# Delta rule, inverse of both directions: products first, then transpositions, then updates

## What is computed

```python
a_kk = jnp.where(strict, jnp.einsum("bhnid,bhnjd->bhnij", k_beta, k) * decay, 0.0)
eye = jnp.eye(c, dtype=q.dtype)
t_inv = lax.linalg.triangular_solve(eye + a_kk, jnp.broadcast_to(eye, a_kk.shape),
                                    left_side=True, lower=True, unit_diagonal=True)
u = jnp.einsum("bhnij,bhnjd->bhnid", t_inv, v * beta[..., None])
w = jnp.einsum("bhnij,bhnjd->bhnid", t_inv, k_beta * jnp.exp(gcum)[..., None])
```

## Time and profile before

| what | us |
|---|---|
| median of 3 runs | 2648.48 |
| lowest and highest of them | 2642.61, 2650.26 |
| span of the profiled execution, first to last instruction | 2645.5 |
| TensorE's busy time in it | 2556.8 |
| layer 0, step 0 levels | some 20 (1854.24 to 1874.16) |

### The profile page before, as it was taken

The page is one execution under the profiler, slowest core; times in us unless marked ns, Lnnn a source line. Parts: engine busy times, 40 slices in busy tenths (PEclk is TensorE's granted clock), DMA queues, the critical chain, the costliest instruction groups (busy, mean ns, idle before and its releaser), DMA issues.

```text
span 2645.5 us, 66516 instructions
## 1 busy us (share of the span) xinstructions
PE 2556.8 (97%) x30782; PEld 2085.4 (79%) x30782; DVE 1269.3 (48%) x1710; ACT 942.9 (36%) x1227; POOL 173.9 (7%) x178
## 2 busy tenths in 40 slices
PE   8999999999999999999999999998999999989999
PEld 7977799897786767767667765687779978877997
DVE  6677655556861000010100101388467857846785
ACT  4455443355540000000000000266545645654663
POOL 1000000000000000000000000202500000160000
PEclk9999999999999999999999999999999999999999
DMA  6445855554459999999999999743035445313443
GB/s 218 142 160 174 307 179 182 152 191 161 149 180 394 407 396 404 412 405 409 398 404 410 405 398 418 287 155 117 31 120 185 171 166 194 105 51 121 171 173 104
DMA packets 94362, 635.37 MB, mean 240 GB/s; under 512 B 11328, under 2 KB 12256, under 8 KB 24320
## 3 DMA queue, kind: packets, MB, share of 16 engines
q1 hardware_dynamic: 85392, 598.61, 59.0%
q0 software_dynamic: 7120, 29.70, 4.0%
q10 hardware_dynamic: 1568, 2.75, 0.3%
HBM read 626.17 MB, written 13.24 MB: 242 GB/s over the span
## 4 chain that ended last, share of the span: by engine, by line
PE 79%; DVE 11%; ACT 5%; issue 3%; DMA 3%; SPq 0%; DVEq 0%; ACTq 0%
PE ps L1032 31%; PE ps L756 13%; PE ps L758 13%; PE ps L757 13%; DVE wlo L1946 3%; DMA raw<-in_units_dram 3%; ACT whi L1481 2%; PE ps L1331 1%; ACT s L1829 1%; PE ps L1310 1%; PE ps L1342 1%; DVE s L2306 0%; DVE mx L2268 0%; DVE x L2381 0%; PE ps L964 0%
## 5 line engine op out<-in xcount | busy, mean ns | idle before, releaser
L1946 DVE TENSOR_TENSOR wlo<-raw,whi 128x2048 fp32r<-128x2048 f32 (+5 forms) x250 | 531.6, 2135 | 306.5 <-ACT whi L1481 306.0
L1032 PE MATMUL ps<-raw,xe 128*32 128x256 f32 x10752 | 585.3, 379 | 5.5 <-DMA raw<-in_units_dram 4.7
L1032 PEld LDWEIGHTS ps<-raw,xe 128*32 128x32 f32 x10752 | 391.1, 110 | 194.5 <-DMA raw<-in_units_dram 7.0
L1481 ACT ACTIVATE whi<-raw 128x2048 fp32r<-128x2048 f32 (+4 forms) x252 | 447.8, 1780 | 203.7 <-PE ps L758 188.8
L756 PE MATMUL ps<-xTh,whi 128*128 128x256 f32 x1480 | 418.1, 283 | 0.0
L758 PE MATMUL ps<-xTh,wlo 128*128 128x256 f32 x1480 | 417.4, 282 | 0.0
L757 PE MATMUL ps<-xTl,whi 128*128 128x256 f32 x1480 | 417.3, 282 | 0.0
L2489 DVE TENSOR_TENSOR hb<-ps,hb 128x384 f32<-128x384 f32 x56 | 31.2, 558 | 777.5 <-ACT hb L1656 777.5
L1032 PE MATMUL ps<-raw,hTe 128*32 128x256 f32 x5376 | 291.8, 379 | 3.5 <-issue 3.5
L756 PEld LDWEIGHTS ps<-xTh,whi 128*128 128x128 f32 x1480 | 279.1, 189 | 0.8 <-issue 0.7
L757 PEld LDWEIGHTS ps<-xTl,whi 128*128 128x128 f32 x1480 | 278.8, 188 | 0.1
(11 more groups left out here) (582 smaller groups left out, 3229.7 us busy)
## 6 DMA issues: line engine op xcount, KB each, us to landing
raw<-in_units_dram SPq DMA_DIRECT2D x544, 1024.0 KB, 7.7
raw<-in_units_dram SPq DMA_DIRECT2D x18, 512.0 KB, 3.5
raw<-in_units_dram SPq DMA_DIRECT2D x6, 768.0 KB, 6.9
raw<-in_units_dram SPq DMA_DIRECT2D x8, 544.0 KB, 3.6
raw<-in_units_dram SPq DMA_DIRECT2D x6, 688.0 KB, 4.0
g<-in_b_gate_dram POOLq DMA_DIRECT2D x16, 256.0 KB, 9.2
raw<-in_units_dram SPq DMA_DIRECT2D x4, 576.0 KB, 4.5
rows_y<-yb ACTq DMA_DIRECT2D x7, 288.0 KB, 6.4
```

The costliest lines, as they stand in the source:

```text
L1032: ins = self.e.matmul(bands(ps[r:r + 32, 256 * i:256 * i + 256]), G.x[:, kk, o:o + 32], w[:, k, :, c:c + 128], start=(kk == 0 and i != 1), ...
L1481: self.e.activation(self.m.hi[u % NHL][:, 0:n], self.m.raw[u % NRAW][:, 0:n], ACT.Copy) \
L1946: self.e.tensor_tensor(self.m.lo[u % NHL][:, 0:n], self.m.raw[u % NRAW][:, 0:n], self.m.hi[u % NHL][:, 0:n].bitcast(F32), ALU.subtract) \
```

## The change

The transposition `tr` becomes a step of its own behind the products of both directions. TensorE's queue in a level is then product 0, product 1, transposition 0, transposition 1, update 0, update 1. ScalarE's copies follow: `q` of 0, `q` of 1, `T` of 0, `T` of 1. VectorE, GpSimd and SyncE have nothing in the step `tr`. No instruction is added or taken away, and no semaphore wait changes its condition; the PSUM buffers are handed out in the new order.

```diff
@@ Plan.delta
-                o += [("lq", k) + c for c in K]
+                o += [("lq", k) + c for c in K] + [("tr", k) + c for c in K]
@@ Tensor.do
-        elif what in ("dd", "de", "kq", "gram", "qkT", "t0", "lq", "lu", "du", "s1", "s2"):
+        elif what in ("dd", "de", "kq", "gram", "qkT", "t0", "lq", "tr", "lu", "du", "s1", "s2"):
@@ Tensor.delta_inverse
                 ins = e.matmul(ps[half(a_), span(512 * c + 64 * r_)], m.E[d][r, s], TT[r, s], start=True, stop=True)
-            ins.then_inc(*self.up("mm_delta", ("full",) + key))
-            key = ("tr",) + a
+        elif what == "tr":
             ps = self.fill(key, ("T", k) + K)
             ins = self.turn_pairs(lambda r_: ps[:, span(128 * r_, 128)], TT)
@@ Scalar.do
-        elif what in ("dd", "de", "kq", "qkT", "t0", "lq", "du", "s2"):
+        elif what in ("dd", "de", "kq", "qkT", "t0", "lq", "tr", "du", "s2"):
```

## The result

| what | before | after |
|---|---|---|
| median of 20 runs, us | 2647.30 | 2654.32 |
| lowest and highest, us | 2642.61, 2651.72 | 2650.23, 2657.43 |
| span of the profiled execution, us | 2645.5 | 2654.2 |
| TensorE's busy time in it, us | 2556.8 | 2552.1 |

The ratio is 1.0025 with a 95% interval of 1.0020 to 1.0031: about 6.6 us slower (7.0 by the medians). Forecast were 3.2 us and a time of 2651.7. The time lies in the range and inside the 0.3% called no change, but the interval excludes a ratio of 1, and the size is twice the one forecast. That the time came within 2.6 us is in part luck: the forecast was counted from 2648.48, the median of three runs, and the median of the twenty is 2647.30.

What follows compares the result with a forecast made beforehand. TensorE's queue up to update 0 and the chain behind it were taken as the bound. Step 0 (1.07 and 0.77) and step 1 twice (1.36) made 3.2 us: 2648.48 to 2651.7 us, range 2644.5 to 2658.5.

Steps and rivals of the forecast that it cites:

- the ordinary level: Levels behind a step's first: ScalarE's copy sets update 0 at 2.62, so a level takes 4.12 us, 0.19 more.
- The first level: First level of a step: product 1 waits for `TT` of direction 1, update 0 comes 0.53 us later.
- the queue's saving of 0.34: TensorE's queue per level: two fewer tiling mode changes at 0.17 us each, left unused because ScalarE's copy comes last.
- step 0: Levels of step 0: 1.07 us longer in layer 0, 0.77 in layer 1.
- levels 2 and 3 nothing: Step 1, each layer: level 1 costs 0.30 us, levels 2 and 3 nothing, 4 and 5 0.19 each, 0.68 together.
- the halt gives back: Step 1: instruction halts of 0.65 and 0.81 us shrink by whatever a level loses inside a halted stretch.
- 3.62 us of a packet's way: Step 1: TensorE runs out of instructions, and an instruction packet's way takes at least 3.62 us.
- rival 1: All levels: the instruction supply hides the whole loss, time stays at 2648.5 us; chance 0.14.
- rival 2: All levels: saved mode changes count, 6.8 us less, or 1.6 less (2646.9) with the supply's floor; chance 0.06.
- rival 3: VectorE's subtractions stay 0.80 us apart, delaying product 1; each level loses 0.37, total 2657 us; chance 0.10.
- rival 4: TensorE's clock falls to 1.2 GHz because levels have idle gaps: 30 us more, 2682 us; chance 0.04.

Runs made afterwards that it cites:

- e7: All levels ordered product 0, transposition 0, transposition 1, product 1, against the kernel before: 2649.61 us, ratio 1.0009.
- e5: Changed kernel with only level 3 of step 1 back in the old order: 2650.49 us, ratio 1.0015 to the kernel before.
- e2: Kernel before with the new order in step 1 of both layers only: 2650.49 us, ratio 1.0012.
- e6: Kernel before with only level 3 of step 1 in the new order: 2652.97 us, ratio 1.0021.
- e9: Kernel before with only TensorE's queue in the new order, ScalarE's copies in the old: 2659.55 us, ratio 1.0037.
- e8: Kernel before with only ScalarE's copies in the new order, TensorE's queue in the old: 2661.26 us, ratio 1.0052.
- e4: Changed kernel with 32 repeated `du` products shifting the instruction blocks: 2653.95 us, ratio 1.0023 to the kernel before.
- e3: Kernel before with 32 repeated `du` products shifting the instruction blocks: 2651.61 us, ratio 1.0018 to the unshifted one.
- e1: Kernel before with the new order in step 0 of both layers only: 2648.91 us, ratio 1.0004.

## Why the prediction was right for a level, wrong on the halts and half in size

**Right: the ordinary level.** Forecast 4.12 us with product 1 0.61 behind product 0, ScalarE's second copy pair from about 1.95 on, update 0 at 2.62 released by ScalarE. Measured 4.10 to 4.11, 0.60, 1.91, 2.58 and `[0.51 <-ACT W]`. The idle time there is 0.51 and not 0.4. The first level: 4.48 us where 3.97 + 0.53 = 4.50 was worked out, with 0.37 idle where 0.35 was said. Of the queue's saving of 0.34, e7 shows one half as a price (0.17 fewer at the one place where a product now follows a product); as forecast, it is unused in after.

**Off in size: step 0.** Forecast 1.07 and 0.77, measured 0.76 and 0.11. In layer 1 the levels 1 to 4 did lengthen (by 0.08 and three times 0.18), but level 5 and what follows it took 9.51 us against 10.02; 0.5 came back there. In layer 0 the same stretch gave 0.3 back. What came back is for the most part a halt that the prediction did not see. It took step 0 to be free of halts from level 3 alone; in level 5 of before TensorE runs out of instructions in update 0, 0.52 us in layer 1, and 0.16 in update 1 in layer 0 (1873.54). Neither halt is there after:

```profile
2343.73 0.68 PEld L1342 LDWEIGHTS ps<-Q,W 64*64 64x64 f32 x35 [0.52 <-issue]
```

**Wrong: "levels 2 and 3 nothing" and what a level loses inside a halted stretch, "the halt gives back".** This term was 0.68 in each layer's step 1 and measured 2.49 and 1.70. The halts did not shrink, they grew. The 3.62 us of a packet's way was taken as a fixed pace; it is two parts, the time until the packet sets out and the 2.2 to 2.9 us from there (3.35 once, in e5). The first is 1.14 to 1.92 us behind the resumption after nearly all halts of over 0.3 us in the levels of the eleven kernels, and 2.86 to 2.91 in the other nine cases.

Shown is: these nine are level 3 of step 1 in after, e2, e6 and e9, in both layers, and in e8 in layer 0; it is not late in before, e5 and e4. So it takes the boundary at that place and a wait for ScalarE ahead of update 0, which the new order brings and e8 brings without it. Taking it away (e5) gave back 1.7 us in each layer; bringing it in alone (e6) cost 1.18 and 0.41.

Argued only: why. In all nine the packet sets out 0.92 to 1.01 us behind the end of that wait (in after it ends at 1906.88 and 2381.48), so it looks as if TensorE asks for the next block only once it has got past a certain instruction, and stands at the wait ahead of it. In e4 the boundary lies 32 products earlier in level 3, and the packet leaves at 1903.26, before that wait (it ends at 1904.39). Layer 1 of e8 is the limit of this account: its wait lies as far behind the resumption as in layer 1 of after, by the recorded instructions to within one or two, and its packet isn't late. Which instruction it is, and whether it is one, stays open.

The Trainium skill says on the page "Runtime: NRT & Kernel Launch", section "Instruction fetch mechanics", that the next page of instructions is fetched while the current one runs and that this is mostly hidden. In these levels it is not: one row has 1.44 us of it.

**Missing: the stretch from `du` to step 1's first product.** It was not in the sum and measured 0.16 and 1.39. In layer 1 after:

```profile
2359.21 1.60 POOL L3112 TENSOR_TENSOR R<-A,mk 128x512 f32<-128x512 f32 x1
2359.60 1.75 DVE L2794 SCALAR_TENSOR_TENSOR gm<-gm,mk 128x512 f32<-128x512 f32 x1
...
2361.41 1.01 PEld L1304 LDWEIGHTS ps<-mk,gm 64*64 64x64 f32 x32 [1.26 <-DVE gm L2794]
```

VectorE's first masking (line 2794) takes 1.75 us beside GpSimd's (line 3112, from 2359.21), and TensorE waits 1.26 us for it. In before the same instruction took 0.68 us, and GpSimd's began 0.27 behind it; the second took 1.75 to 1.76 in either.

```profile
2353.55 0.68 DVE L2794 SCALAR_TENSOR_TENSOR gm<-gm,mk 128x512 f32<-128x512 f32 x1
...
2353.82 1.54 POOL L3112 TENSOR_TENSOR R<-A,mk 128x512 f32<-128x512 f32 x1 [1.34 <-PE ps L1310]
```

Which of the two begins first varies from kernel to kernel: the stretch took 7.96 or 7.97 us in layer 1 of after, e3, e4, e8 and e9, and 6.6 to 6.9 in before, e1, e2, e5, e6 and e7. e3 has the old order throughout, e1 and e5 have the new one in the step 0 ahead of the stretch. So these 1.4 us are in the profiled execution's difference, but they aren't shown to be the change's; they depend on when the engines arrive.

**The rivals.** The supply as the cover of everything (rival 1) is refuted by step 0, where each of levels 2 to 4 is 0.18 longer, with no halt in them to take it up; in level 5 it did cover some, as said. The saved mode changes as gain (rival 2) did not come; ScalarE's queue covers them, as said, and e7 shows that the supply would have taken a part. The subtractions 0.80 apart (rival 3) fell: product 1 is 0.60 behind. The clock (rival 4) fell too. The windows view of two stretches after, columns as in the earlier trace rows:

```profile
1855.20:1876.00 20.80, 17.85 (x673) 15.56 (x677) 7.45 (x13) 11.94 (x23) 13.23 (x11) 1.00 0.06 20
1889.47:1915.80 26.33, 19.70 (x813) 17.66 (x810) 8.54 (x17) 11.15 (x21) 14.60 (x12) 1.00 0.02 4
```

TensorE is busy 17.85 of 20.80 us and 19.70 of 26.33, and the granted clock is 1.00 in both, the level of 2.4 GHz. In the first level of some other kernels it was lower, as said under the table of lengths; in after it was not.

None of the orders tried was shown faster than the kernel before; e1 (1.0004) and e7 (1.0009) come nearest.

The range held partly by luck: step 0 was put 0.97 us too high and step 1 2.83 too low, and the 1.55 between `du` and step 1 were not in the sum.

## What to carry to other kernels

When several small chains share two engines, price the order by the instruction that starts the longest tail (here update 0, with 1.5 us behind it), not by the queue's total: grouping equal operations put another chain's product and copy in front of it. Before counting on slack from instruction halts, look at when the instruction packets set out and not only at their mean distance; a changed order, or a new wait alone, can make them later. And a forecast of a few tenths of a per cent has to include the joints around the changed stretch, since two engines that meet or miss each other there were worth 1.4 us here, beside a change of 6.6.

## What the runs showed of the hardware that was not expected

- An instruction packet set out 1.14 to 1.92 us after TensorE resumed from a halt in the levels, and 2.86 to 2.91 in nine cases in which TensorE stood at a semaphore wait shortly behind the resumption (after, e2, e6, e8, e9); in a tenth such case (e8, layer 1) it set out after 1.15. The block ran 2.2 to 2.9 us after its packet (3.35 once). Two neighbouring resumptions were 3.5 to 4.3 us apart in the one case and 5.25 to 5.63 in the other.
- A VectorE operation of 128 x 512 with two tensor operands took 0.68 us alone or where GpSimd's operation of the same size began behind it, and 1.75 where GpSimd's had begun first; GpSimd's took 1.27 alone and 1.54 to 1.81 beside it in the stretches shown. The Trainium skill, page "GPSIMD Engine Reference", section "1. Specifications", says that the two share their SBUF interfaces and contend when VectorE reads two inputs there; the rows agree.
- A change between 64 x 64 products and full 128 x 128 transposes on TensorE cost 0.17 us: 0.46 from one group of 32 products to the next, 0.63 to a group of transposes. The Trainium skill's page "TensorEngine Tiling (Array Packing)", section "Key Properties", says that changing the mode drains the engine; e7 agrees (0.46 from product 1 to update 0).
